# Expert row buffers that hold four slots of 32 tokens instead of one slot of 128

## The reference, cut to what matters

```
qd = (xb @ w_query).astype(f32).reshape(-1, PEER_HEADS, 2, PEER_DQ // 2)
...
top_s, pos = lax.top_k(cand, PEER_TOPK)
idx = jnp.take_along_axis(cand_idx, pos, axis=-1)
g = jax.nn.softmax(top_s, axis=-1)
u = expert_down[idx]
act = jax.nn.gelu(jnp.einsum('thkd,td->thk', u, xb).astype(f32), approximate=False)
return jnp.einsum('thk,thkd->td', (g * act).astype(xb.dtype), expert_up[idx])
```

## Time and profile before

| What | Value |
|---|---|
| three runs | 4394.46, 4400.70, 4415.16 us |
| span of the profiled execution | 4384.4 us |
| up to the first product of the first tile | 1443 us |
| from there to the last gathered slot | 2887 us |
| last part, with the 8 single tokens | 54 us |
| TensorE busy, share of the span | 3487.9 us, 80% |
| VectorE | 2354.8 us, 54% |
| GpSimd | 1348.0 us, 31% |
| ScalarE | 1050.6 us, 24% |

### The profile page before, as it was taken

The page is one execution under the profiler, slowest core; times in us unless marked ns, Lnnn a source line. Parts: engine busy times, 40 slices in busy tenths (PEclk is TensorE's granted clock), DMA queues, the critical chain, the costliest instruction groups (busy, mean ns, idle before and its releaser), DMA issues.

```text
span 4384.4 us, 39661 instructions
## 1 busy us (share of the span) xinstructions
PE 3487.9 (80%) x11633; PEld 1922.7 (44%) x11633; DVE 2354.8 (54%) x4730; ACT 1050.6 (24%) x3019; POOL 1348.0 (31%) x1232
## 2 busy tenths in 40 slices
PE   7699996469997687786787788778769778877876
PEld 1698774135555342352353344335325324324432
DVE  0651111746663767457546646646755755664574
ACT  1110112123341222222222222222222222222222
POOL 0020110400000343344444443434444444443442
PEclk9799997689998898898899889889889889988988
DMA  7232210642323899999999999999999999999996
GB/s 273 69 103 110 82 61 31 246 165 86 101 72 134 345 374 374 381 384 366 361 389 368 376 375 379 366 370 380 382 384 378 381 374 383 377 375 375 395 382 272
DMA packets 210634, 1269.30 MB, mean 290 GB/s; under 512 B 25875, under 2 KB 51099, under 8 KB 74060
## 3 DMA queue, kind: packets, MB, share of 16 engines
q0 software_dynamic: 159504, 1114.68, 64.3%
q1 hardware_dynamic: 50902, 152.03, 9.9%
HBM read 1218.26 MB, written 48.36 MB: 289 GB/s over the span
## 4 chain that ended last, share of the span: by engine, by line
DMA 26%; PE 25%; issue 8%; ACT 4%; POOL 3%; DVE 3%; POOLq 0%; ACTq 0%; DVEq 0%; SPq 0%
DMA e_buf<-in_experts,e_idx 26%; PE ps L1771 22%; PE ps L1502 3%; POOL e_buf L1738 3%; DVE e_buf L1840 2%; ACT e_wts L1812 2%; ACT e_diag L1816 1%; ACT e_acts L1810 1%; DMA e_buf<-in_experts,e_idxT 0%; DMA r_wq<-in_w_query 0%; POOLq L58 0%; DVE r_work L1590 0%; DVE r_row L1591 0%; DVE r_work L1587 0%; DVE r_pos L1550 0%
## 5 line engine op out<-in xcount | busy, mean ns | idle before, releaser
L1771 PE MATMUL ps<-e_buf,e_diag 128*128 128x512 f32 x4096 | 2026.0, 652 | 638.7 <-ACT e_diag L1816 635.2
L1840 DVE SCALAR_TENSOR_TENSOR e_buf<-e_buf,e_h 128x1024 f32<-128x1024 f32 x1024 | 1248.2, 1227 | 1091.6 <-DMA e_buf<-in_experts,e_idx 1075.2
L1738 POOL DMA_INDIRECT e_buf<-in_experts,e_idx x1024 | 1195.4, 1167 | 1605.1 <-PE ps L1771 1406.3
L1771 PEld LDWEIGHTS ps<-e_buf,e_diag 128*128 128x128 f32 x4096 | 836.0, 210 | 1758.4 <-issue 990.9
L1810 ACT ACTIVATE e_acts<-e_dots 128x4 f32<-128x4 f32 x256 | 52.6, 205 | 2085.0 <-DVE e_buf L1840 2076.4
L1816 ACT ACTIVATE e_diag<-ident,e_wts 128x128 f32<-128x128 f32 x1024 | 327.3, 390 | 27.8 <-ACT e_wts L1812 2.7
L1502 PEld LDWEIGHTS ps<-r_h2T,r_wq 128*128 128x128 f32 x2304 | 269.3, 193 | 34.0 <-issue 34.0
L1502 PE MATMUL ps<-r_h2T,r_wq 128*128 128x128 f32 x2304 | 269.9, 276 | 3.1 <-DMA r_wq<-in_w_query 3.1
L830 PE MATMUL ps<-xo_w_out,xo_catT 128*128 128x512 f32 x512 | 224.5, 592 | 1.7 <-DVE xo_x L863 1.7
L1812 ACT ACTIVATE e_wts<-e_acts,e_gate 128x1 f32<-128x1 f32 x1024 | 218.5, 284 | 9.2 <-ACT e_acts L1810 1.1
L74 PE MATMUL ps<-p_wth,hT_high 128*128 128x512 f32 (+1 forms) x432 | 170.6, 395 | 10.9 <-PEq L413 10.9
(11 more groups left out here) (338 smaller groups left out, 3007.2 us busy)
## 6 DMA issues: line engine op xcount, KB each, us to landing
w_mod_sb<-in_w_mod SPq DMA_DIRECT2D x12, 2048.0 KB, 8.4
e_buf<-in_experts,e_idx POOLq DMA_INDIRECT x1024, 9.1
p_wt<-in_w_rows SPq DMA_DIRECT2D x6, 2048.0 KB
proj_d<-p_ev POOLq DMA_DIRECT2D x48, 256.0 KB, 2.3
x_zgv<-proj_d SPq DMA_DIRECT2D x8, 1536.0 KB
p_w<-in_w_chan SPq DMA_DIRECT2D x20, 512.0 KB, 4.3
r_wq<-in_w_query SPq DMA_DIRECT2D x4, 2048.0 KB, 20.2
xbc_d<-p_res POOLq DMA_DIRECT2D x12, 516.0 KB, 3.0
```

Source lines behind the costliest of these rows:

```text
L1738: return pool.indirect_dma_start(out=buf[s][:], out_offset=None, in_=io["experts"], in_offset=bass.IndirectOffsetOnAxis(ap=numbers, axis=0 ...
L1771: last = nc.tensor.matmul(g.bank(cols), diag[:, k % RING, :], buf[k % RING][:, D + cols * 512:D + (cols + 1) * 512], start=(k == 0), stop= ...
L1840: V.scalar_tensor_tensor(out=down, in0=down, scalar=1.0, in1=row, op0=ALU.mult, op1=ALU.mult, accum_out=out).then_inc(sem, 1)
```

## The change

A gather no longer brings one slot of 128 tokens but four slots of 32 tokens: partition 32·s + t of buffer j in a group of four holds slot s of token 32·j + t. The group still brings the same 512 rows, dealt differently. The four buffers of a group now belong to the four quarters of the tokens, and the sum over the partitions that TensorE makes adds up four slots of one quarter at once: the weights are 128x32 (four small diagonals above each other), and the result goes to 32 partitions of the bank, one column group of the array for each buffer. Per group there are eight products as before, of 32 instead of 128 columns of weights, in another order: the first 512 columns of the four buffers, then the second 512. TensorE waits once for all four `weighed`; `summed` is counted up four times, by the last four products.

What goes with it:

- `deal`, a new function, brings numbers and gates from "token by slot" to the new layout with 16 small products for each half of the numbers and of the gates; TensorE gets four more pieces, behind groups 18, 20, 27 and 29 (in the first tile also 6 and 8). VectorE copies the numbers out of TensorE's result memory, ScalarE the gates.
- Each of four buffers `h2[j]` holds the rows of 32 tokens four times. SyncE loads them with 16 transfers a tile of 32 rows of 4 KB, when the last four products of the tile before are through. The copy by VectorE (L1850) goes. The router's own rows are loaded when TensorE has transposed the last ones.
- The phases of the mixer give back their constants before the expert phase begins; their code is the same.

```diff
+        for s in range(GROUP):
+            out = g.ps[s * QUAD:(s + 1) * QUAD, bank * 512 + cols.start:bank * 512 + cols.stop]
+            by_token = out.rearrange("p (q j) -> p j q", j=GROUP)
+            for j in range(GROUP):
+                last = nc.tensor.matmul(by_token[:, j, :], g.ident[:, j * QUAD:(j + 1) * QUAD], by_slot[:, s, :],
+                                        start=True, stop=True)
...
+        for half in range(2):
+            pe.wait_ge(self.chosen, n * 4 + 2 * half + 2)
+            self.deal(self.num, half, 2).then_inc(self.num_ps, 1)
+            yield
+            pe.wait_ge(self.gated, n * 2 + half + 1)
+            self.deal(self.gate, half, 3).then_inc(self.gate_ps, 1)
+            yield
...
-            dve.wait_ge(self.chosen, n * 4 + 2 * half + 2)
-            V.tensor_copy(self.idx[:, ks], self.num[:, ks]).then_inc(self.numbered, 1)
...
+            dve.wait_ge(self.num_ps, n * 2 + half + 1)
+            V.tensor_copy(self.idx[:, ks], self.g.bank(2, cols=SLOTS // 2, at=ks.start)).then_inc(self.numbered, 1)
...
-PE_PIECES = {q: 1 for q in range(1, 14)}
+PE_PIECES = {q: 1 for q in (*range(1, 14), 18, 20, 27, 29)}
...
-        diag = sb("diag", [P, RING, P])
+        diag = sb("diag", [P, RING, QUAD])
...
             def tile(n, first):
-                sp.wait_ge(h2_kept, n + 1)
+                for j in range(GROUP):
+                    if not first:
+                        sp.wait_ge(dotted, n * SLOTS - GROUP + j + 1)
+                    for s in range(GROUP):
+                        sp.dma_start(h2[j][s * QUAD:(s + 1) * QUAD, :],
+                                     g.h2_d[bass.ds(n * P + j * QUAD, QUAD), :]).then_inc(h2_in[j], 16)
+                sp.wait_ge(rt.h2T_ps, n + 1)
                 sp.dma_start(rt.h2[:], g.h2_d[bass.ds(n * P + P, P), :]).then_inc(rt.h2_in, 16)
...
-                for k in range(SLOTS):
-                    if k == 0 and not first:
+                for q in range(NG):
+                    if q == 0 and not first:
                         pe.wait_ge(fin.sum_read, n)
-                    pe.wait_ge(weighed, n * SLOTS + k + 1)
+                    pe.wait_ge(weighed, n * SLOTS + (q + 1) * GROUP)
                     for cols in range(2):
-                        last = nc.tensor.matmul(g.bank(cols), diag[:, k % RING, :],
-                                                buf[k % RING][:, D + cols * 512:D + (cols + 1) * 512],
-                                                start=(k == 0), stop=(k == SLOTS - 1))
-                    last.then_inc(summed, 1)
-                    if k % GROUP == GROUP - 1:
-                        drive(route, PE_PIECES.get(k // GROUP, 0))
+                        for j in range(GROUP):
+                            s = (q * GROUP + j) % RING
+                            out = g.ps[j * QUAD:(j + 1) * QUAD, cols * 512:(cols + 1) * 512]
+                            last = nc.tensor.matmul(out, diag[:, s, :], buf[s][:, D + cols * 512:D + (cols + 1) * 512],
+                                                    start=(q == 0), stop=(q == NG - 1))
+                            if cols:
+                                last.then_inc(summed, 1)
...
-                        A(diag[:, k % RING, :], g.ident[:], ACT.Copy, scale=wts[:, k:k + 1]).then_inc(weighed, 1)
+                        A(diag[:, k % RING, :], eye32[:], ACT.Copy, scale=wts[:, k:k + 1]).then_inc(weighed, 1)
...
-                V.tensor_copy(h2[:], rt.h2[:]).then_inc(h2_kept, 1)
-                dve.wait_ge(h2_kept, n + 1)
                 for k in range(SLOTS):
+                    if k < GROUP:
+                        dve.wait_ge(h2_in[k], n * (16 * GROUP) + 16 * GROUP)
                     dve.wait_ge(landed[k % RING], n * PER + 16 * (k // RING) + 16)
-                    dot(k % RING, h2[:], dots[:, k:k + 1], dotted)
+                    dot(k % RING, h2[k % GROUP][:], dots[:, k:k + 1], dotted)
```

More of the change, by code:

```diff
@@ L47 @@
 GROUP = 4
+QUAD = P // GROUP
 EPS = 1e-6
@@ L120, in __init__, with mixer_constants @@
         self.ident = s("ident", [P, P])
+        self.eye8 = s("eye8", [P, NS, NS])
+        self.iota16 = s("iota16", [P, TOPK])
+        self.eps = s("eps", [P, 1])
+        self.ps = stack.enter_context(nc.psum_tensor("ps", [P, 8 * 512], F32))
+    def mixer_constants(self, stack):
+        s = lambda name, shape: stack.enter_context(self.nc.sbuf_tensor(name, shape, F32))
         self.tri = s("tri", [P, P])
@@ L1476, in load_constants, with deal, tensor @@
                 sp.dma_start(self.keys[:], self.g.io["sub_keys"]).then_inc(self.keys_in, 16)
-    def tensor(self, pe, n):
+    def deal(self, src, half, bank):
+        g, nc = self.g, self.g.nc
+        cols = slice(half * (SLOTS // 2), (half + 1) * (SLOTS // 2))
+        by_slot = src[:, cols].rearrange("p (q s) -> p s q", s=GROUP)
+        for s in range(GROUP):
[4 more added lines that the diff above has]
+                                        start=True, stop=True)
+        return last
+    def tensor(self, pe, n, dealt):
         g, nc = self.g, self.g.nc
         pe.wait_ge(self.h2_in, n * 16 + 16)
+        if dealt is not None:
+            pe.wait_ge(self.numbered, dealt)
+            pe.wait_ge(self.gate_kept, dealt)
         for k in range(KD):
@@ L1538, in scalar @@
             A(self.e[:, hs], self.e[:, hs], ACT.Exp).then_inc(self.e_ready, 1)
+            yield
+            act.wait_ge(self.gate_ps, n * 2 + half + 1)
+            A(self.gate_s[:, half * (SLOTS // 2):(half + 1) * (SLOTS // 2)],
+              g.bank(3, cols=SLOTS // 2, at=half * (SLOTS // 2)), ACT.Copy).then_inc(self.gate_kept, 1)
             yield
@@ L1653, in scalar @@
         act.wait_ge(self.r_ready, n + 1)
-PE_PIECES = {q: 1 for q in range(1, 14)}
[L1658 to L1663, removed]
+PE_PIECES = {q: 1 for q in (*range(1, 14), 18, 20, 27, 29)}
+ACT_PIECES = {q: 1 for q in (2, 4, 6, 7, 9, 10, 12, 13, 14, 18, 21, 26, 30)}
+DVE_PIECES = {8: 2, 9: 3, 11: 2, 12: 3, 13: 2, 14: 2, 15: 2, 16: 2, 17: 4, 19: 1, 20: 4, 21: 3, 22: 3, 23: 3,
+              24: 3, 25: 4, 26: 3, 27: 1, 29: 1}
+FIRST_PE_PIECES = {6: 1, 8: 1}
+FIRST_ACT_PIECES = {6: 1, 9: 1}
+FIRST_DVE_PIECES = {0: 4, 1: 4, 2: 4, 3: 4, 4: 3, 5: 3, 7: 1, 9: 1}
 def drive(pieces, count):
@@ L1805, in tile @@
                         gs = slice(half * HALF_SLOTS, (half + 1) * HALF_SLOTS)
-                        act.wait_ge(rt.gated, n * 2 + half + 1)
-                        ch.step(A(gate[:, gs], rt.gate[:, gs], ACT.Copy))
+                        act.wait_ge(rt.gate_kept, n * 2 + half + 1)
+                        ch.step(A(gate[:, gs], rt.gate_s[:, gs], ACT.Copy))
                     ks = slice(q * GROUP, (q + 1) * GROUP)
@@ L1897, in build, with mixer @@
         g = Prog(nc, stack, io)
+        with ExitStack() as mixer_mem:
+            g.mixer_constants(mixer_mem)
+            mixer(nc, g)
+        g.phase(experts)
+def mixer(nc, g):
         with ExitStack() as st:
```

31 lines of the change are left out of this document (19 added, 12 removed).

## The result

The changed kernel takes 4561.0 us (median of four runs, 4559.2 to 4566.9), the kernel before 4403.2 us beside it: 1.0364 times, 95% interval 1.0345 to 1.0384. It is slower, as forecast, and within the range, but by 158 us where 88 were forecast. The profiled execution spans 4557.7 us, 173 more than before; from the first product to the last gathered slot it takes 3061.3 us where it took 2887.3. The 174 us all lie in the ring. (The profiled execution of the kernel before was some 15 us shorter than its median, that of the changed kernel was not; so 174 us of this pair stand for the 158 of the medians.)

What follows compares the result with a forecast made beforehand. A turn of the ring, not one engine or transfer, bounds the kernel; 88 - 24 + 25 - 5 + 4 = plus 88 us on 4384.4 gives 4472, with 16.3 us to the median 4489 us; range for 8 in 10 4315 to 4640.

Steps and rivals of the forecast that it cites:

- The wait for four weights: TensorE waits for all four of ScalarE's weights before a burst: plus 0.55 us to every release.
- The burst: TensorE's 16 matmuls for a group's eight products: 9 places taken, first buffer released after 6, every burst cold without router pieces.
- 9 places: Estimated burst length on TensorE, in matmul times of 0.44 us warm or 0.85 cold, with matmuls beginning in program order.
- The rival: Four column groups on TensorE run side by side: burst of 4 places, first release after 4; 4351 us, chance 0.33.
- Five of 0.85 and one of 0.44: Cold burst on TensorE up to the first release: 4.69 us, 1.28 us more than 3.41.
- The gathers "as fast as it can": GpSimd issues gathers 1.25 us apart; 6.68 us from gather to product, the other three landing 2.45 us apart, 7.35 us.
- The turn then: Ring turns without router pieces: 23.3 and 22.9 us, 1.0 us more a turn, plus 88 us over 88 turns.
- Turns with router pieces: Five ring turns a tile: minus 0.6 us each, 40 turns, minus 24 us (minus 48 to plus 40).
- My cold value of 23.3 us: Length of a ring turn with router pieces if its burst is cold; a warm one was put at 21.1 us.
- The tokens' rows: SyncE's loads of 2 MB a tile instead of a copy on chip: plus 25 us (0 to 34).
- The small terms: One deal ahead of the first gather, plus 4 us; VectorE's copy gone, minus 5 us; dealing in the loop, nothing.

Runs made afterwards that it cites:

- after: The changed kernel itself, against the kernel before: 4561.0 us, 1.0364 times.
- lot_by_lot: The changed kernel with the two loops around its products turned, so both products of one gathered buffer stand behind each other: 4560.0 us, 1.0366 of the kernel before.
- slot_warm: The changed kernel with a wait for each weight by itself and dummy matmuls behind VectorE's products to keep the clock up: 4441.4 us, 1.0114 of the kernel before.
- h2_once: The changed kernel with the tokens' rows loaded for the first tile alone: 1.0167 of the kernel before.
- wait_slot: The changed kernel with TensorE waiting for each buffer's weight by itself, not once for all four: 1.0193 of the kernel before.
- late_release: The kernel before, still with 128x128 weights, but with the changed product order and the one wait for four weights: 1.0790 of the kernel before.
- h2_lots: The changed kernel with the tokens' rows written to memory four times over, each lot loaded by one plain transfer of 128 rows: 4535.9 us, 1.0290 of the kernel before.
- h2_bcast: The changed kernel with each lot of the tokens' rows loaded by one broadcast transfer that reads its 32 rows four times: 1.0733 of the kernel before.

## Why the forecast was right, and where it was not

The direction and the range held; the picture of the burst did not. The prediction said that it would be wrong if the burst were 3.5 us cold, and the burst was 3.6 us cold. The number stood because two errors cancel in the turn and two misses beside it, of 62 and 59 us, still fit into a wide range: that is luck, not mechanism.

- **The wait for four weights**: plus 0.55 us forecast. From the fourth landing to the burst it is 2.99 us before and 3.53 after in the far groups. Right.
- **The burst** ("9 places", first release after 6): wrong. No run shows either number, they were an estimate; the runs showed four places, with the first release behind the fourth. The rival was right here, and lot_by_lot shows that the assumed order did not bind: with another order in the program its burst took 3.66 us. The places themselves were priced right: 0.85 us at a granted 0.50 and 0.43 at 1.00, in the trace before as in after and slot_warm. "Five of 0.85 and one of 0.44" no run of the new products shows: in after's far groups the burst is 3.58 us on the mean, four of 0.85. To the first gather 7.8 us, not 9.31 and 8.90: 1.3 us too many.
- **The gathers "as fast as it can"**: they came so (1.25 us apart when nothing held GpSimd), but the 14.03 us from the first gather to the fourth product (6.68 + 7.35) were too few. In the far groups the fourth landing comes 7.30 + 2.86 + 2.65 + 2.52 = 15.33 us behind the first gather. The three followers' distances are those of before (2.80, 2.65, 2.52); gathers sent closer together (1.65, 1.51 and 1.38 us apart after; 2.10, 1.72 and 1.69 before) did not land closer. My two turns before were lucky ones: their mean is 22.12 us, that of the far groups 22.41.
- **The turn then**: the two errors cancel, by luck. 23.3 and 22.9 us forecast, 23.20 measured. The rival with four places had the burst right and the time wrong by the same 14.03 us: with 15.33 its turn of 22.1 us is 23.4.
- **Turns with router pieces**: minus 0.6 us forecast, plus 0.97 measured. I let a share of the bursts be warm; 81% of them are above 3 us, hence cold (3.6 us at a granted 0.50, 1.92 at 1.00), where before most took 7.03 to 7.13 us, warm. My cold value of 23.3 us would have served (23.04), with the same two errors in it.
- **The tokens' rows** (25 us, 0 to 34): the term that was missed by most, 87 us with h2_once. I priced bytes at the saturated pace and looked for a wait on VectorE, which is hardly there (11.2 us); the cost is a slower pace at a full share.
- **The small terms** (plus 4 us for the deal ahead of the first gather, minus 5 for the copy): the first product comes 1.0 us later than before. No run priced the copy, or the dealing inside the loop, by itself.

Without the rows the sum holds by parts: the turns of h2_once are 0.63 us longer than before on 88 turns and 0.87 us on 40, 55 + 35 = 90 us; its stretch is 87 us longer. Against the forecast of 88: rows 62 us more, router turns 59 more, far turns 33 less, which makes 176 of the measured 174. The direction stands on causes that the runs showed: the first release comes later (wait_slot gives back 81 us, late_release prices it on the old kernel), the tokens' rows cost 87 us, and the shorter products do not buy that back. At a granted 0.50 a burst takes 3.6 us; with it at full clock, 1.92 us, and the wait parted, the far turn is 22.43 us, that of the kernel before and no less. What holds it there stays open, since the dummies themselves delay the burst.

## What to carry to other kernels

In a ring of buffers, price a change by when the first buffer comes free, by how fast the next gathers can be started behind it, and by the mean landing time over many turns, not by the busy time of the engine that gets faster: here TensorE lost 1132 us of work and the kernel 158 us. Join waits only where the first of the joined items was not already setting the pace; parting them gave back 81 us here (wait_slot). Before tokens or weights are copied over several partition ranges, look at the GB/s, not the share, of the stretch in which they come (294 to 332 GB/s at a share of 1.02 or 1.03 in after); here one plain transfer over all partitions, from a source laid out for it, was the cheaper form, by 37 us (h2_lots).

## What the runs showed of the hardware

- Products of 32 columns on four column groups ran side by side: 16 matmuls in 1.92 us at full clock (slot_warm), where the burst of 128 columns took 7.13, 3.7 times, its matmuls beginning one by one, 0.43 us apart; at half clock 3.64 us (after). With the lots' products in the other order the burst took 3.66 us (lot_by_lot).
- With bursts of 3.6 us every 11.6 us the granted clock was 0.50 in the window from 3234.80 and 0.65 over the ring; all 112 far bursts took over 3 us (after).
- Four transfers of 32 rows of 4 KB, into 32 partitions each, came to 245 ns a packet (after); one plain transfer of 128 such rows over 128 partitions gave 162 over all packets of 4 KB (h2_lots). Packets of the gathers beside them took 371 and 324 ns. The share of busy time was 1.02 to 1.03 and 0.96 to 1.01.
- A broadcast of four copies as the leading dimension had four landings a lot, not sixteen, moved 57 to 203 GB/s at a tile's start, and the ring took 170 us more than with the four transfers a lot that it replaced (h2_bcast).
- Gathers of 1 MB started 1.4 to 1.7 us apart landed 2.5 to 2.9 us apart, no closer than those started 1.7 to 2.1 us apart (after and before, far groups).
